# Expert weights in three transfers of 4 MB instead of six of 2 MB

## What is computed

```python
def clamped_swiglu_expert(xb, w_gu, b_gu, w_down, b_down):
    gu = xb @ w_gu + b_gu                         # (n, 1024) @ (1024, 2048)
    gate = jnp.minimum(gu[:, :D_FF], SWIGLU_LIMIT)
    up = jnp.clip(gu[:, D_FF:], -SWIGLU_LIMIT, SWIGLU_LIMIT)
    act = (up + 1.0) * (gate * jax.nn.sigmoid(gate * SWIGLU_ALPHA))
    return act @ w_down + b_down                  # (n, 1024) @ (1024, 1024)
```

## Time and profile before

| | us |
|---|---|
| median of 3 executions | 1278.38 |
| lowest and highest | 1274.4, 1279.73 |
| profiled execution | 1279.26 |
| its span, first to last instruction | 1276.6 |
| TensorE busy in it | 1185.5 (93%) |
| VectorE busy | 727.2 (57%) |
| ScalarE busy | 566.7 (44%) |
| GpSimd busy | 443.9 (35%) |

### The profile page before, as it was taken

One profiled execution on the slowest core, in us unless ns is written; L12 is line 12 of the kernel. 1 busy time (PEld: TensorE's weight loads), 2 busy tenths in 40 slices (PEclk: granted clock), 3 DMA queues, 4 the chain that ended last, 5 costly groups with the idle time before them and its releaser, 6 DMA issues.

```text
span 1276.6 us, 46573 instructions
## 1 busy us (share of the span) xinstructions
PE 1185.5 (93%) x12042; PEld 558.4 (44%) x12043; DVE 727.2 (57%) x3075; ACT 566.7 (44%) x4248; POOL 443.9 (35%) x2636
## 2 busy tenths in 40 slices
PE   6999999999899988989998999999998788999985
PEld 5875455856344433333343444444443223333333
DVE  2237766555666645645565666666665445666454
ACT  3135666333444444434453544555544334544340
POOL 0000003000354443534453455544444333555341
PEclk9999999999999999989999999999999989999997
DMA  5142125257779999999999989999999999999994
GB/s 186 40 133 66 34 53 162 89 222 328 316 327 411 430 426 427 426 425 428 425 426 426 426 358 402 407 402 407 401 409 427 427 426 427 428 426 381 428 426 185
DMA packets 53190, 427.68 MB, mean 335 GB/s; under 512 B 13168, under 2 KB 25760, under 8 KB 28576
## 3 DMA queue, kind: packets, MB, share of 16 engines
q1 hardware_dynamic: 50976, 427.07, 81.2%
q10 hardware_dynamic: 2176, 0.13, 0.1%
HBM read 424.63 MB, written 2.36 MB: 334 GB/s over the span
## 4 chain that ended last, share of the span: by engine, by line
PE 64%; DMA 23%; DVE 6%; SPq 2%; issue 2%; ACT 1%; DVEq 1%; ACTq 0%; POOL 0%; POOLq 0%
PE PS L1105 29%; DMA W<-in_expert_w_gate_up 22%; PE PS L1121 15%; PE PS L698 14%; PE HTP L698 3%; DVEq L219 1%; SPq L229 1%; DVE ACC L1569 1%; SPq L239 0%; PE HTP L1161 0%; SPq L233 0%; DMA W<-in_norm_mix_w 0%; PE HTP L874 0%; PE HTP L708 0%; DVE AT L1545 0%
## 5 line engine op out<-in xcount | busy, mean ns | idle before, releaser
L1105 PE MATMUL PS<-W,XT 128*32 128x512 f32 x5184 | 597.4, 610 | 65.1 <-DMA W<-in_expert_w_gate_up 59.0
L1105 PEld LDWEIGHTS PS<-W,XT 128*32 128x32 f32 x5184 | 167.9, 111 | 440.5 <-issue 340.2
L667 ACT ACTIVATE XG<-HTP 128x6 f32 x2592 | 259.6, 181 | 155.8 <-issue 155.8
L435 POOL TENSOR_TENSOR ACC<-ACC 128x8 f32 x1296 | 225.7, 215 | 265.2 <-DVE ACC L1565 265.2
L1121 PE MATMUL PS<-W,AT 128*32 128x256 f32 x5184 | 299.5, 383 | 3.9 <-DVE ACC L1565 3.9
L425 POOL COPY XG<-HTS 128x2 f32 x1296 | 199.9, 212 | 252.6 <-DVE XT L1527 246.2
L1121 PEld LDWEIGHTS PS<-W,AT 128*32 128x32 f32 x5184 | 174.0, 112 | 153.8 <-issue 60.4
L698 PE MATMUL PS<-W 128*128 128x512 f32 (+3 forms) x680 | 220.5, 479 | 3.3 <-ACT W L620 1.1
L677 ACT ACTIVATE SIG<-GU 128x256 f32<-128x256 f32 x81 | 33.9, 418 | 352.5 <-DVE GU L1534 352.5
L1569 DVE TENSOR_TENSOR ACC<-ACC 128x8 f32 x1296 | 161.4, 187 | 13.9 <-issue 1.3
L698 PEld LDWEIGHTS PS<-W 128*128 128x128 f32 (+1 forms) x680 | 124.9, 192 | 76.9 <-issue 66.5
(11 more groups left out here) (273 smaller groups left out, 623.8 us busy)
## 6 DMA issues: line engine op xcount, KB each, us to landing
W<-in_expert_w_gate_up SPq DMA_DIRECT2D x128, 2048.0 KB, 24.9
W<-in_expert_w_down SPq DMA_DIRECT2D x64, 2048.0 KB, 17.4
W<-in_w_in SPq DMA_DIRECT2D x10, 1024.0 KB, 5.8
W<-in_x SPq DMA_DIRECT2D x8, 512.0 KB, 11.2
W<-in_w_out SPq DMA_DIRECT2D x2, 1024.0 KB, 9.9
W<-in_w_out SPq DMA_DIRECT2D x1, 2048.0 KB, 7.9
RAW<-in_expert_b_gate_up SPq DMA_DIRECT2D x128, 2.0 KB
out<-W SPq DMA_DIRECT2D x4, 512.0 KB, 2.6
```

Of the source, the lines that this page charges most:

```text
L435: ins = g.tensor_tensor(col, col, YTV[:, :, HALF + m:HALF + m + 1], ALU.add)
L667: ins = a.activation(XGK[:, 0:KP, m:m + 1], HTP[:, :, bass.ds(toks[m], 1)], ACT.Copy)
L1105: last = pe.matmul(GPS[32 * j:32 * j + 32, :].rearrange("p (g n) -> p g n", g=2), XT[:, 32 * k:32 * k + 32], rhs, start=(k == 0), stop=(k ...
```

## The change

From the third expert on, `reload` issues gate-up weights in two halves of 4 MB (four parts k, 32 KB contiguous per partition) in place of four quarters of 2 MB (16 KB per partition), and the down weights in one transfer of 4 MB (32 KB per partition) in place of two. The first half of the gate-up weights is issued once `gu_read1` allows it, the second once `gu_ps` does, the down weights once `d_ps` does. TensorE waits for half 0 at k = 0 and for half 1 at k = 4, and for all down weights at k = 0 of the down product. Experts 0 and 1 are still loaded in quarters and halves as before, but two transfers now count on one semaphore, so that each threshold rises by 16.

```diff
             def gu_part(e, p, parts, through=None):
...
-                                 w_gu[e].rearrange("(p k) n -> p k n", p=P)[:, 2 * q:2 * q + 2, :]).then_inc(S_(f"gu_in{p}{q}"), 16)
+                                 w_gu[e].rearrange("(p k) n -> p k n", p=P)[:, 2 * q:2 * q + 2, :]).then_inc(S_(f"gu_in{p}{q // 2}"), 16)
             def dn_part(e, p, parts, through=None):
...
-                                 w_dn[e].rearrange("(p k) n -> p k n", p=P)[:, 4 * q:4 * q + 4, :]).then_inc(S_(f"dn_in{p}{q}"), 16)
+                                 w_dn[e].rearrange("(p k) n -> p k n", p=P)[:, 4 * q:4 * q + 4, :]).then_inc(S_(f"dn_in{p}"), 16)
...
             def reload(at, p):
                 through = sp.value_load(LASTB[0:1, bass.ds(at - 2, 1)], min_val=0, max_val=MAXB - 1) + 1
                 e = sp.value_load(ORDER[0:1, bass.ds(at, 1)], min_val=0, max_val=NE - 1)
-                gu_part(e, p, range(4), through)
+                for h in range(2):
+                    sp.wait_ge(S_("gu_read1" if h == 0 else "gu_ps"), through)
+                    sp.dma_start(GUW[p][:, 4 * h:4 * h + 4, :],
+                                 w_gu[e].rearrange("(p k) n -> p k n", p=P)[:, 4 * h:4 * h + 4, :]).then_inc(S_(f"gu_in{p}{h}"), 16)
                 sp.wait_ge(S_("y_free"), at - 1)
                 gu_bias(e, p)
                 dn_bias(e, p)
-                dn_part(e, p, range(2), through)
+                sp.wait_ge(S_("d_ps"), through + 1)
+                sp.dma_start(DNW[p], w_dn[e].rearrange("(p k) n -> p k n", p=P)).then_inc(S_(f"dn_in{p}"), 16)
...
                 for k in range(KD):
-                    if first_of_expert and k % 2 == 0:
-                        pe.wait_ge(S_(f"gu_in{p}{k // 2}"), rnd)
+                    if first_of_expert and k % 4 == 0:
+                        pe.wait_ge(S_(f"gu_in{p}{k // 4}"), rnd + 16)
...
             def down(i, p, rnd):
...
-                pe.wait_ge(S_(f"dn_in{p}0"), rnd)
+                pe.wait_ge(S_(f"dn_in{p}"), rnd + 16)
                 for k in range(KD):
-                    if k == KD // 2:
-                        pe.wait_ge(S_(f"dn_in{p}1"), rnd)
```

## The result

| | before | changed |
|---|---|---|
| median of 17 executions, us | 1277.16 | 1282.87 |
| lowest, highest | 1273.51, 1284.97 | 1281.12, 1286.71 |
| profiled execution (its span) | 1279.26 (1276.6) | 1281.72 (1279.9) |

The ratio is 1.0048 with a 95% interval of 1.0034 to 1.0061: the changed kernel is 0.48% slower, 5.7 to 6.1 us. Forecast were +3.0 us and a range of 1273.5 to 1289.5. The two profiled executions lie only 3.3 us apart in span: the first took 2.1 us more than the median of its kernel and the second 1.15 us less. The ratios leave out one execution of 3548.87 us, in experiment 5, the only one that took over 1.5% more than the fastest of its kernel.

What follows compares the result with a forecast made beforehand. A chain alternating between TensorE and DMA, with three DMA parts of 510 us, was taken to set the end. Terms 0 + 0 + 5.9 + 0.5 - 3.4 = +3.0 us gave 1281.4 us, range 1273.5 to 1289.5.

Steps and rivals of the forecast that it cites:

- (a): SyncE: three fewer waits and issues per expert save some 1.4 us, but its queue stands before y_free; worth 0.
- (b): Weight issues: permission to load comes later, half 0 by 1.7 us, yet still in time for the queue; worth 0.
- (c): Three hand-backs: last gate-up half starts late, with more work and slower clock behind the landing; +5.9 us (3.0 to 10.8).
- (d): Expert 0's down product waits at k=0 for all of its weights; +0.5 us on the chain.
- (e): DMA parts: 32 KB runs take 0.67% less than 16 KB ones; -3.4 us over 510 us (0 to -6.8).
- C: Rival: the queue cuts 32 KB runs, rate stays, late halves as forecast; +6.4 us, 1284.8; chance 0.13.
- D: Rival: each transfer in a row has 0.15 us fixed cost, merging saves 7.8 us, 1273.6; chance 0.05.
- B: Rival: at hand-backs half clock covers last half and down product, tight experts wait; 1289.7 to 1293.2 us; chance 0.22.
- A: The forecast itself: late halves cost a few us against cheaper runs; 1281.4 us, range 1275 to 1286; chance 0.60.

Runs made afterwards that it cites:

- experiment 5: Kernel before, with late waits (two quarters awaited together) except at places 13, 14, 25, 26 and 31, among them the hand-backs: 1280.47 against 1279.05 us, ratio 1.0015.
- experiment 2: Kernel before with only the down weights in one 4 MB transfer, gate-up still in quarters: 1277.88 against 1278.57 us, ratio 0.9996.
- experiment 4: Changed kernel with the last gate-up half split again into two 2 MB quarters with own waits: 1278.33 against 1278.57 us before, ratio 0.9999.
- experiment 1: Kernel before, six 2 MB transfers kept, but TensorE waits for two quarters together at k=0 and k=4: 1287.04 against 1278.57 us, ratio 1.0081.
- experiment 3: Changed kernel with down weights back in two 2 MB transfers, only gate-up halves left: 1283.30 against 1278.57 us before, ratio 1.0046.
- experiment 6: Changed kernel with all gate-up weights of an expert in one 8 MB transfer: 1292.38 against 1279.05 us before, ratio 1.0106.
- experiment 7: Changed kernel plus 16 zero matmuls in the last expert's stand before k=4: 1279.11 against 1279.05 us before; rerun 1278.86 against 1278.98, ratio 1.0013.
- experiment 8: As experiment 4, but gate-up parts 6 and 7 in 1 MB transfers with own waits: 1274.85 against 1279.05 us before, ratio 0.9963.
- experiment 9: As experiment 8, but no run over 16 KB, seven transfers an expert: 1276.70 against 1278.98 us before, ratio 0.9987.
- experiment 10: As experiment 8, but down weights in two 2 MB halves with waits at k=0 and k=4: 1273.39 against 1278.98 us before, ratio 0.9976.

## Why the prediction came out as it did

**What bounds the kernel** held: the chain changes sides at the same six places, DMA parts and TensorE parts alternate, the two TensorE parts between hand-back and down issue took 239.0 and 83.6 to 83.7 us in both traces, and experiment 5 shows that stands elsewhere cost little.

**(a), (b)** cost nothing, as forecast. SyncE's queue still stands at y_free, no new dry spot came, and the experts between 750 and 944 don't wait for weights.

**(c)** carried the change, as forecast, with 5.9 us. In the profiled execution it measured 0.02 + 3.54 + 1.27 = 4.8 us. The first hand-back, 1.7 forecast, gave nothing there. The step took a stand of 6.4 us before every last half. But the late half of the expert at place 10 pushed the start of place 13 from 686.66 to 689.71 while its data came 1.95 us sooner, so that the stand was only 2.69 us; and the clock stayed up. That the shorter stand is the reason is likely and not shown. In the repeat of the same kernel the stand there was 3.63 us:

```profile
698.16 5.34 PE L1109 MATMUL PS<-W,XT 128*32 128x512 f32 x32 [3.63 <-DMA W<-in_expert_w_gate_up]
703.32 3.64 PE L1123 MATMUL PS<-W,AT 128*32 128x256 f32 x64
```

That is 8.6 us from landing to next block, the +1.7 of the forecast. This execution took 1285.83 us instead of 1281.72. The hand-back is 1.7 us of the 4.0 that the spans differ by; 2.3 us arose before the experts' DMA parts begin, where the change has no part yet but (d): the down issue came at 399.77 instead of 397.43. Over all 14 traces of this document it came between 395.6 and 399.8, whatever the kernel. One place can be seen, the last block of expert 0:

```profile
335.31 8.77 PE L1109 MATMUL PS<-W,XT 128*32 128x512 f32 x64 [1.88 <-DVE XT L1529]
```

In the first execution these 64 took 7.07 us, behind the same stand. The second hand-back was forecast at +3.4 and gave 3.54, the third at +0.8 and gave 1.27.

**What the sum left out** is the end. Behind the last hand-back come two stands, for VectorE (3.89 us) and GpSimd (4.23), which were there before. The work behind them took 5.35 us each before, 6.17 and 6.10 after; with what follows, the way from the last down product to the end grew by 1.86 us, from 18.9 to 20.8. Not all of that is shown to be the change: experiments 2 and 4, which end with a quarter, have 19.8 us there, experiment 5 has 19.0, and the four other traces in which all experts start late and nothing was added (experiments 1, 3, 6 and the repeat) have 20.7 to 20.9. So the late half costs some 0.9 to 1.9 us behind the last hand-back. The prediction priced the half clock only up to the hand-back's down product and let the tail stand as it was, without a reason; that is the step that failed. The added matmuls of experiment 7 brought one of the two back to 5.35. Why the slow stretch of the other stayed at 6.2 is open.

**(d)** was forecast at 0.5 us, from a landing at 342.2. The new wait is there, with 0.94 us; in the repeat, where the block in front of it took 8.77 us, there is none. Issue and block both came 1.1 us sooner in this execution (333.06 instead of 334.22), so the product starts when it did before; what the wait cost by itself the two traces can't say better than that:

```profile
341.54 3.66 PE L1123 MATMUL PS<-W,AT 128*32 128x256 f32 x64 [0.94 <-DMA W<-in_expert_w_down]
```

**(e)** was forecast at -3.4 us from a line through three run lengths. The DMA parts shrank by 2.06 + 0.68 + 0.86 = 3.6 us, and the window went to 430 GB/s where 429 to 430 stood in the text. Times agree: late waits without long runs cost 8.5 us (experiment 1), with them 4.6 to 5.7. The same line holds within 0.8 us in the traces of the experiments. The last column is what it gives for 510 us, 8.1 ns for each run more or fewer:

| kernel | share of the weights by run length | DMA parts, us | against before | by the line |
|---|---|---|---|---|
| before | all 16 KB | 513.6 | | |
| experiment 1 | all 16 KB | 513.5 | -0.1 | 0 |
| experiment 2 | 1/3 in 32 KB | 512.6 | -1.0 | -1.1 |
| experiment 3 | 2/3 in 32 KB | 510.9 | -2.6 | -2.3 |
| experiment 4 | 2/3 in 32 KB | 511.0 | -2.6 | -2.3 |
| changed, repeat | all 32 KB | 510.0, 509.5 | -3.6, -4.1 | -3.4 |
| experiment 6 | 1/3 in 32 KB, 2/3 in 64 KB | 508.3 | -5.3 | -4.5 |
| experiment 8 | 2/3 in 32 KB, 1/6 in 8 KB | 512.3 | -1.2 | -1.2 |
| experiment 9 | 1/6 in 8 KB | 514.7 | +1.1 | +1.1 |
| experiment 10 | 1/3 in 32 KB, 1/6 in 8 KB | 513.5 | 0.0 | 0 |

Traces with the same transfers differ by up to 0.9 us (513.5 to 514.1 with experiment 5; 509.1 to 510.0 with the two runs of experiment 7). The window of experiment 6 reads 429 GB/s where the line gave 431 (the same window reads 430 in the changed kernel), so the window alone does not show the gain; its DMA parts do. One thing the experiments can't separate: every weight transfer here has 128 runs, 8 for each engine, so a cost of 8.1 ns a run is the same as one of 0.065 us a transfer. For a cost per run speak the rows with 1 KB and 4 KB runs.

Of the rivals, C is out by the packet count. D put 0.15 us on each transfer in a row, 7.8 us in all, beside the 3.4 of the runs; the DMA parts shrank by 3.6 us and not by 11.2, and experiment 9, with one transfer an expert more than before, has them 1.1 us longer, all of it explained by its 8 KB runs. So at that size D is out. The Trainium skill's page "DMA: Bandwidth & Descriptors" (Anatomy of one DMA) has some 2 us fixed for a DMA that GpSimd issues; those here come from SyncE, and an overhead of that kind shows only on an empty queue (8.0 us for 2 MB, 4.9 us of data at 427 GB/s). The prediction's estimate from that page would not have taken DMA off the chain, as it says: 3 x 11.6 = 34.8 us an expert is more than the 29.5 that DMA takes here. B's mechanism, slow clock over more of the work, was part of why the result lies on the slow side of the forecast; its other parts, runs no cheaper and tight experts that wait, didn't happen. A's own range took 7.5 us as the most for (c) where the bounds of (c) went to 10.8, and gave no reason.

The mechanism of the forecast held, and the size of its sum was too small: +3.0 against a measured 5.7 to 6.1 us. That the profiled pair shows 3.3 is luck: the tail (+1.9) and the first hand-back (forecast at +1.7, not there in that execution) nearly cancel. With the first hand-back as in the repeat, the terms as measured are 0.02 + 1.7 + 3.54 + 1.27 + 1.86 for TensorE, -3.6 for DMA and 0.2 for the rest, 5.0 us; the remaining 1 us or so stays open.

## What to carry to other kernels

A transfer's size is also the grain in which its reader may start. In a kernel in which DMA and TensorE take turns at the front, count the places where DMA hands over, and multiply them by the work that is left behind the last landing. Here large pieces where nobody waits and small ones last (experiments 8 and 10) beat one size for all, by 0.2 to 0.4%. And price work behind a stand at the clock that it will get, not at the one that the same work has elsewhere.

## What the hardware showed that had not been expected

- The fixed part of a run in the DMA queue, 8 ns as worked out from three rates, is small but real: 356, 410, 427 and 430 GB/s at 1, 4, 16 and 32 KB, and DMA parts of 513.6, 510.0 and 508.3 us with 16 KB, 32 KB and mostly 64 KB.
- In the changed kernel the granted clock stood at 0.50 for 6.8 us at the third hand-back and again behind the wait for VectorE:

```profile
1243.80:1250.60 6.80, 4.84 (x24) 1.19 (x28) 0.99 (x9) 0.00 (x0) 0.97 (x6) 0.50 1.06 445
1257.40:1264.20 6.80, 5.08 (x48) 2.72 (x52) 3.43 (x23) 0.00 (x0) 2.80 (x16) 0.50 0.00 1
```

  Before, the stretch behind the same wait for VectorE was 3.4 us long (1258.2 to 1261.6, clock 0.51), though the one at the third hand-back was longer, 10.2 us.
- A stand of 2.69 us at 696 left the clock at full speed and one of 3.63 us at 698 didn't, in two executions of the same kernel, a difference of 1.7 us of work. But the length of the stand alone does not decide it: before the change a quarter behind 2.97 us (at 1000.41) took 1.92 us and one behind 2.75 us (at 970.92) took 3.19, and in experiment 9 a stand of 1.57 us was enough.
- The part ahead of the first down issue of the DMA parts, in which the kernels hardly differ, took 395.6 to 399.8 us in the 14 traces. That is as much as most of the differences that these experiments measure.
